# The last feed-forward network's output: seven block products in place of eight

## The chip, the cores and the metric

One core of one Trainium2 chip runs the whole kernel in one launch. The metric is the device time of that launch in microseconds (us). The profile is one profiled execution; times inside it count from its first instruction.

## The reference

One transformer-like layer over 512 latent tokens and 256 context tokens, 1024 features wide:

```
x  = x + position embedding
x  = LN(a*x + 0.5*gate*swiglu(modulate(x)))      # network 1, context tokens too
x  = LN(a*x + gate*mixer(modulate(x), context))  # gated linear attention and HGRN2, both directions
x  = LN(a*x + 0.5*gate*swiglu(modulate(x)))      # network 2, latent tokens: the change is here
swiglu(h) = (silu(h @ Wg) * (h @ Wu)) @ Wout     # 1024 -> 2816 -> 1024
```

All in float32, with `a` = 2 ** 0.25; `gate` is one row of 1024 factors, applied to the output columns. So the last network computes hid (512 x 2816) times Wout (2816 x 1024).

## The kernel before

All of it is one list of weight jobs (`weight_jobs`, `JOBS`), which every engine walks in the same order: network 1 for latent tokens (`L1`), for context tokens (`C`), the mixer, then network 2 for latent tokens (`L2`). A matmul operand in float32 is split in a high part (float32r) and a low part, the rest; a product is three matmuls, low x high, high x low and high x high (`product`, L1962 to L1964).

A weight job goes through four engines. SP loads 1 MB (or 0.75) into one of two raw buffers (`load`; buffer i % 2, as soon as VectorE has made the low part of job i - 2). ScalarE copies the high part (`split_hi`, L839) into one of three slots, when TensorE is done with the job before in that slot. VectorE subtracts for the low part (`split_lo`, L1291). TensorE waits for the low part (`ready`).

Network 2 ran in two parts of 11 hidden tiles (`FFN_PARTS`). An inner job ("in") computes gate and up columns of one tile of 128 hidden features for 512 tokens: 48 matmuls of 512 columns into a pair of PSUM banks. ScalarE takes the silu (L899), VectorE multiplies (L1462), ScalarE copies the high part (L904) and VectorE the low part (L1468) of the hidden tile. Then the output jobs ("out") of that part: for each half of the 1024 output columns, three steps of 3, 4 and 4 k tiles, and in each step all four token tiles (`out_half`). VectorE multiplies a finished bank by the gate row (L1406) and adds it to `xl` (`add_output`, L1412, L1414). For the last half the gate was multiplied into the raw weights instead (`gate_weights`, L1301), and TensorE took the tiles in an order of their own (`LAST_ORDER`, `last_half`), so that each tile's statistics (L1343, L1346), centring (L1384), scaling (L1391) and store can follow while TensorE works on the next.

The order on each engine is written out by hand, and an engine waits in order: what stands behind a waiting instruction waits too. GpSimd's queue is idle in this stage. PSUM has eight banks of 512 floats; the inner jobs use 0 to 3 (and 4 for one early tile).

Of the kernel before, what the change touches and what calls it, by code (L numbers as in the profile page):

```python
# [38 lines left out]
FFN_PARTS = {"L1": (11, 11), "C": (22,), "L2": (11, 11)}  # L46
OUT_STEPS = {11: (3, 4, 4), 22: (4, 4, 4, 4, 3, 3)}
LAST_ORDER = [(0, 0), (0, 1), (0, 2), (0, 3), (1, 0), (1, 1), (2, 0), (2, 1), (1, 2), (2, 2), (1, 3), (2, 3)]
# [11 lines left out]
def weight_jobs():  # L60
# [3 lines left out]
    def ffn(tag):  # L64
        for part, tiles in enumerate(FFN_PARTS[tag]):
            jobs.extend((tag, "in", part, j) for j in range(tiles))
            jobs.extend((tag, "out", part, half, s) for half in range(2) for s in range(len(OUT_STEPS[tiles])))
# [33 lines left out]

USES = [sum(slot_of(j) == slot_of(i) for j in range(i)) for i in range(len(JOBS))]
# [11 lines left out]


def gated(i):

    return i < len(JOBS) and JOBS[i][:4] == ("L2", "out", 1, 1)
# [27 lines left out]
def out_keys(tag):  # L146

    tiles = TC if tag == "C" else TL
    return [(tag, part, half, i) for part in range(len(FFN_PARTS[tag])) for half in range(2) for i in range(tiles)]

# [41 lines left out]
def build(nc, t, out):  # L192

    with ExitStack() as ctx:
# [8 lines left out]
        h_hi = sb("h_hi", [P, KT, TOK], F32R)  # L203
        h_lo = sb("h_lo", [P, KT, TOK], F32R)
# [29 lines left out]
        with ExitStack() as s0:  # L234
# [7 lines left out]
            with ExitStack() as s3:  # L242
# [22 lines left out]
                with ExitStack() as s1:  # L265
                    hid_last = [sb(f"hid_{x}_last", [P, 11, W], F32R, s1) for x in ("hi", "lo")]
                    gate_last = sb("gate_last", [KT, P], F32, s1)
# [7 lines left out]
        for block in (xc, gain_bias_b):  # L275
            ada_slots.append(block[:, :, :].rearrange("p a (b c) -> p (a b) c", c=256))
        sums = small[:, 0:3 * (TL + TC)].rearrange("p (a b) -> p a b", b=3)
# [33 lines left out]

        gate_dram = nc.dram_tensor("gate_rows", (4, KT, P), F32, kind="Internal").ap()
# [60 lines left out]
        def hidden_of(tag):  # L373

            return {"L1": hid_lat, "C": hid_ctx, "L2": hid_last}[tag]
# [60 lines left out]

        def weight_size(i):

            key = JOBS[i]
            if key[1:2] == ("out",):  # L440
                return out_k(key[0], key[2], key[4])[1] * W
            return {"LR": KT * 32, "mix": SLOT // 2, "early": SLOT // 2}.get(key[0], SLOT)

        def weights(i):
# [3 lines left out]
            if JOBS[i] == ("LR",):  # L448
                return (raw[i % 2][:, 0:KT * 32],) + tuple(x[s][:, 0:KT * 96] for x in (hi, lo))
            return tuple(x[:, 0:weight_size(i)] for x in (raw[i % 2], hi[s], lo[s]))  # L450
# [19 lines left out]
        s_smask = sem("scan_mask_loaded")  # L470
# [4 lines left out]
        s_ones = sem("ones_loaded")  # L475
# [22 lines left out]
        s_sum = sem("centred_squares_summed")  # L498
# [19 lines left out]
        s_fmod = sem("first_h_tile_modulated")  # L518
# [18 lines left out]
        s_a2hi = sem("a2_hi_ready")  # L537
# [11 lines left out]
        s_ez = sem("gla_exp_ready")  # L549
# [3 lines left out]
        s_le = sem("forget_log_ready")  # L553
# [7 lines left out]
        s_eq = sem("exp_q_ready")  # L561
        s_ei = sem("exp_k_ready")
        s_ex = sem("exp_tail_ready")
        s_fac = sem("chunk_factors_ready")
# [20 lines left out]
        s_gated = sem("last_half_weights_gated")  # L585
        s_se = sem("silu_exp_ready")
        s_sc = sem("silu_exp_plus_one_ready")
        s_sl = sem("silu_log_ready")
# [9 lines left out]
        w2o = t["ffn2_w_out"].rearrange("(k p) n -> p k n", p=P)  # L598
        wmi = t["w_mix_in"].rearrange("(k p) n -> p k n", p=P)
# [19 lines left out]

        block = ctx.enter_context(nc.Block())  # L620
# [3 lines left out]
        def _(sp):  # L624
            def load(i, pieces=2):
                key, s = JOBS[i], i % 2
                raw = weights(i)[0]
                if i >= 2:
                    sp.wait_ge(s_lo[slot_of(i - 2)], USES[i - 2] + 1)
                if key[0] == "V" and key[1] == 0:  # L630
                    pass
                if key[1:2] == ("in",):
# [6 lines left out]
                    return  # L639
                if key[1:2] == ("out",):  # L640
# [3 lines left out]
                    src, c0, width = (w2o if tag == "L2" else w1o), half * W, W  # L644
# [42 lines left out]
            sp.dma_start(smask[:, :], t["k_smask"][:, 0:SEQ]).then_inc(s_smask, 16)  # L687
# [15 lines left out]
            for i in range(4, len(JOBS)):  # L703
# [6 lines left out]
                if key == ("mo", 0, 1):  # L710

                    sp.wait_ge(s_ex, n2(len(GROUPS) - 1, 1))
# [18 lines left out]
        def _(pool):  # L731
# [25 lines left out]
            pool.wait_ge(s_smask, 16)  # L757
# [28 lines left out]
            def state_queries(g, d):  # L786

                pool.wait_ge(s_qdec, n2(g, d))
                pool.wait_ge(s_fac, n2(g, d))
# [27 lines left out]

        @block.scalar
        def _(act):
            def wait_done(i):  # L820
                act.wait_ge(s_done[slot_of(i)], USES[i] + 1)

            def split_hi(i):
# [10 lines left out]
                if gated(i):  # L834
                    act.wait_ge(s_gated, JOBS[i][4] + 1)
# [12 lines left out]
            def centred_std(what, stream, s, i):  # L848
# [3 lines left out]
                nc.scalar.activation(between_sq[:, :], x_of(stream, i), ACT.Square, bias=mv[:, c, 0:1], scale=-1.0,  # L852
                                     accum_out=mv[:, c, 1:2]).then_inc(s_sum, 1)
                act.wait_ge(s_sum, n - STAT["post", "ctx", 0, 0] + 1)
# [33 lines left out]
            def ffn(tag):  # L888
# [3 lines left out]
                for part, tiles in enumerate(FFN_PARTS[tag]):  # L892
                    for j in range(tiles):
                        i, idx = JOB[tag, "in", part, j], HID[tag, part, j]
                        if i not in (0, L2_FIRST):
# [11 lines left out]
                    for half in range(2):  # L907
                        for s in range(len(OUT_STEPS[tiles])):
                            split_hi(JOB[tag, "out", part, half, s] + 2)
                            between(tag, b)  # L910
                            b += 1

# [79 lines left out]
            for pair in range(4):  # L992
# [4 lines left out]
                for k in (2 * pair, 2 * pair + 1):  # L997
                    if k >= 2:
                        act.wait_ge(s_hk, k - 1)
                    nc.scalar.activation(mod_k[:, k % 2, :], xnT[:, k, :], ACT.Identity, bias=mods[:, KT + k, 0:1],  # L1000
                                         scale=scale1[:, k, 0:1]).then_inc(s_fmod, 1)
                    act.wait_ge(s_fmod, k + 1)
# [55 lines left out]
            def forget_sigmoid(g, d):  # L1058
                act.wait_ge(s_e1, FG[g, d] + 1)
                nc.scalar.activation(X0, X0, ACT.Ln).then_inc(s_le, 1)  # L1060
                act.wait_ge(s_le, FG[g, d] + 1)
# [14 lines left out]
            def gla_log(g, d):  # L1076
                act.wait_ge(s_abs, Z[g, d] + 1)
                nc.scalar.activation(X0, X0, ACT.Exp, scale=-1.0).then_inc(s_ez, 1)
                act.wait_ge(s_ez, Z[g, d] + 1)
# [1534 lines left out]
```

## Time and profile before

| | us |
|---|---|
| runs, median of 3 (lowest, highest) | 1347.28 (1345.25, 1348.06) |
| span of the profiled execution | 1344.9 |
| TensorE busy (share of the span) | 1323.4 (98%) |
| VectorE busy | 801.2 (60%) |
| ScalarE busy | 517.5 (38%) |
| GpSimd busy | 74.2 (6%) |

TensorE is PE in the views, its weight loads PEld, VectorE is DVE, ScalarE is ACT, GpSimd is POOL, SyncE is SP; an engine's name with a q is its queue issuing DMAs. Matmuls overlap, so their starts tell the pace better than their durations.

### The profile page before, as it was taken

What the parts mean: (1) busy time and instruction counts of PE and PEld (TensorE: products, weight loads), DVE (VectorE), ACT (ScalarE), POOL (GpSimd) and SP (SyncE); (2) the same over time, 40 slices, a digit from 0 to 9 for tenths busy, and PEclk for the clock granted to TensorE, in tenths of its full rate; (3) what the DMA queues carried; (4) which work ended last, traced back from release to release, by engine and by line L of the source; (5) the groups of instructions that cost most, each with busy time, mean ns of one, the idle gap of its engine ahead of it and who ended that gap; (6) DMA issues with size and microseconds to landing.
All of it is one profiled execution on the core that took longest, in us unless ns stands there. A gap on an engine that the chain in (4) does not pass through costs nothing.

```text
span 1344.9 us, 17714 instructions
## 1 busy us (share of the span) xinstructions
PE 1323.4 (98%) x7200; PEld 1116.1 (83%) x7200; DVE 801.2 (60%) x1146; ACT 517.5 (38%) x718; POOL 74.2 (6%) x83
## 2 busy tenths in 40 slices
PE   8999999999999999999999999999999999999997
PEld 5778888888889999888888788887898888888886
DVE  5546588666777776565136878777863333433356
ACT  5535211222213544566235655556652231222211
POOL 1000000000000000000001111110000000000000
PEclk8999999999999999999999999999999999999999
DMA  9965545665455676552022112123335333333211
GB/s 319 285 177 175 195 151 157 190 186 180 151 178 147 190 188 189 173 172 94 23 79 64 48 48 63 48 64 114 107 85 159 94 103 97 96 101 105 86 63 63
DMA packets 206400, 175.00 MB, mean 130 GB/s; under 512 B 6906, under 2 KB 175464, under 8 KB 206320
## 3 DMA queue, kind: packets, MB, share of 16 engines
q1 hardware_dynamic: 197816, 142.74, 36.6%
q0 software_dynamic: 7808, 29.46, 6.6%
q10 hardware_dynamic: 696, 1.68, 0.4%
q8 instruction: 57, 0.93, 0.3%
q14 instruction: 23, 0.19, 0.0%
HBM read 171.74 MB, written 2.11 MB: 129 GB/s over the span
## 4 chain that ended last, share of the span: by engine, by line
PE 89%; DVE 5%; ACT 3%; issue 2%; DMA 1%; ACTq 0%; DVEq 0%; SPq 0%
PE ps L1962 28%; PE ps L1964 27%; PE ps L1963 27%; PE ps L2001 1%; DVE w_lo L1291 1%; PE ps L2413 1%; PE ps L2398 1%; DMA w_raw<-ffn_w_in 1%; PE ps L2161 0%; PE ps L2014 0%; PE ps L2432 0%; PE ps L2184 0%; DVE xl L1384 0%; DVE xl L1433 0%; PE ps L2205 0%
## 5 line engine op out<-in xcount | busy, mean ns | idle before, releaser
L1962 PE MATMUL ps<-h_hi,w_lo 128*128 128x512 f32 (+1 forms) x1120 | 391.4, 349 | 2.1 <-DVE h_lo L1584 1.0
L1964 PE MATMUL ps<-h_hi,w_hi 128*128 128x512 f32 (+1 forms) x1120 | 387.8, 346 | 0.0
L1963 PE MATMUL ps<-h_lo,w_hi 128*128 128x512 f32 (+1 forms) x1120 | 387.6, 346 | 0.0
L1291 DVE TENSOR_TENSOR w_lo<-w_raw,w_hi 128x2048 fp32r<-128x2048 f32 (+1 forms) x107 | 237.1, 2218 | 169.8 <-ACT w_hi L839 169.7
L839 ACT ACTIVATE w_hi<-w_raw 128x2048 fp32r<-128x2048 f32 (+1 forms) x107 | 198.3, 1854 | 344.9 <-PE ps L1964 315.4
L1962 PEld LDWEIGHTS ps<-h_hi,w_lo 128*128 128x128 f32 x1120 | 211.7, 189 | 32.5 <-issue 5.3
L1964 PEld LDWEIGHTS ps<-h_hi,w_hi 128*128 128x128 f32 x1120 | 211.7, 189 | 26.9
L1963 PEld LDWEIGHTS ps<-h_lo,w_hi 128*128 128x128 f32 x1120 | 211.8, 189 | 25.5
L1313 DVE SCALAR_TENSOR_TENSOR ada_row<-ada_block,c_cols,ada_row 128x256 f32<-128x256 f32 x224 | 108.6, 485 | 8.0
L1462 DVE TENSOR_TENSOR glu<-ps,glu 128x512 f32<-128x512 f32 (+1 forms) x66 | 39.4, 598 | 123.0 <-ACT glu L899 123.0
L1962 PE MATMUL ps<-h_hi,half_lo 128*128 128x512 f32 (+1 forms) x272 | 102.0, 375 | 0.7 <-ACT beside_lo L1123 0.4
L1964 PE MATMUL ps<-h_hi,half_hi 128*128 128x512 f32 (+1 forms) x272 | 97.6, 359 | 0.0
L1963 PE MATMUL ps<-h_lo,half_hi 128*128 128x512 f32 (+1 forms) x272 | 97.4, 358 | 0.0
L899 ACT ACTIVATE glu<-ps 128x512 f32<-128x512 f32 (+1 forms) x66 | 33.9, 514 | 146.8 <-PE ps L1964 146.8
L1962 PE MATMUL ps<-w_hi,hid_lo_lat 128*128 128x512 f32 x176 | 69.6, 396 | 0.0
L1964 PE MATMUL ps<-w_hi,hid_hi_lat 128*128 128x512 f32 x176 | 68.6, 390 | 0.0
L1963 PE MATMUL ps<-w_lo,hid_hi_lat 128*128 128x512 f32 x176 | 68.5, 389 | 0.0
L1962 PE MATMUL ps<-w_hi,hid_lo_last 128*128 128x512 f32 x176 | 68.5, 389 | 0.0
L1963 PE MATMUL ps<-w_lo,hid_hi_last 128*128 128x512 f32 x176 | 68.5, 389 | 0.0
L1964 PE MATMUL ps<-w_hi,hid_hi_last 128*128 128x512 f32 x176 | 68.5, 389 | 0.0
L1962 PEld LDWEIGHTS ps<-h_hi,half_lo 128*128 128x128 f32 x272 | 51.3, 189 | 10.4 <-issue 2.8
L1962 PE MATMUL ps<-w_hi,h_lo 128*128 128x512 f32 x144 | 57.0, 396 | 1.4 <-DVE w_lo L1291 1.4
(273 smaller groups left out, 1770.9 us busy)
## 6 DMA issues: line engine op xcount, KB each, us to landing
w_raw<-ffn_w_in SPq DMA_DIRECT2D x124, 512.0 KB, 5.3
w_raw<-ffn_w_out SPq DMA_DIRECT2D x60, 512.0 KB, 4.2
ada_block<-w_ada POOLq DMA_DIRECT2D x28, 1024.0 KB, 5.8
half_raw<-w_mix_in SPq DMA_DIRECT2D x48, 256.0 KB, 3.3
ada_block<-w_ada SPq DMA_DIRECT2D x6, 1024.0 KB, 9.5
w_raw<-ffn_w_in SPq DMA_DIRECT2D x32, 128.0 KB, 6.1
w_raw<-w_mix_in SPq DMA_DIRECT2D x8, 512.0 KB, 4.2
w_raw<-ffn_w_out SPq DMA_DIRECT2D x12, 256.0 KB, 4.1
```

Source lines behind the costliest of these rows:

```text
L839: nc.scalar.activation(hi, raw, ACT.Copy).then_inc(s_hi[s], 1)
L899: nc.scalar.activation(glu[:, j % 2, 0:n], ps[:, hidden_bank(tag, part, j), 0:n], ACT.Silu).then_inc(s_silu, 1)
L1291: nc.vector.tensor_tensor(lo, raw, hi.bitcast(F32), ALU.subtract).then_inc(s_lo[s], 1)
L1313: ins = nc.vector.scalar_tensor_tensor(out=row, in0=ada_block[:, k, :], scalar=c_cols[:, k, v:v + 1], in1=row, op0=ALU.mult, op1=ALU.add)
L1462: nc.vector.tensor_tensor(hf, ps[:, hidden_bank(tag, part, j) + 1, 0:n], hf, ALU.mult).then_inc(s_hf, 1)
L1962: nc.tensor.matmul(dst, s_low, m_high, start=start, stop=False)
L1963: nc.tensor.matmul(dst, s_high, m_low, start=False, stop=False)
L1964: return nc.tensor.matmul(dst, s_high, m_high, start=False, stop=stop)
L2001: ins = nc.tensor.matmul(ada_sums_ps[:, j, v, :], ada_row[:, v, c], ones[:, 0:2], start=True, stop=True)
L2398: ins = nc.tensor.matmul(ps[p0:p0 + pn, 5, slot * P:(slot + 1) * P], ktok[:, j, p0:p0 + pn], vtok[:, tile, v], start=j != 1, stop=j != 0, ...
L2413: ins = nc.tensor.matmul(ps[:, o_bank(g, hd), c], St[p0:p0 + pn, order(d).index(tile), :], QST[d][p0:p0 + pn, c], start=d == 0 and tile == ...
```

## The change

The output product of network 2 is cut in 2 x 2 x 2 blocks: two token halves, two halves of the 2816 hidden features, two halves of the 1024 columns. In place of the eight block products (A11 B11 + A12 B21 and so on) it computes seven, by the scheme of Strassen and Winograd, from sums of blocks:

- All 22 inner jobs run first; `hid_last` keeps the hidden tiles as plain float32, without the split in two.
- Activation sums are made by VectorE in place: one subtraction of 256 columns with each inner job from the twelfth on, and nine subtractions of up to 1024 elements (`left_n2`, `left_s4`, `left_s3`) during the first products.
- Weight sums (`WEIGHT_SUMS`, four of them, 1408 x 512 floats each) are made in device memory: GpSimd issues four plain copies and four accumulating DMAs from the third inner job on, each waiting for those it needs. SP waits for a sum's semaphore before it loads its first piece.
- Each product has three steps of 4, 4 and 3 k tiles and two token tiles: 21 jobs. For each job ScalarE and VectorE split both the left block (`left_high`, `left_low`) and the weights.
- P1 with P6, P7 and P4 accumulate one after another in one pair of banks (4, 5), P5 with P3 in another (6, 7), P2 in a third (0, 1). Between them ScalarE copies P1, P5 and P3's banks out (`keep`), and VectorE adds or subtracts what a pair of banks holds to these copies (`join`, `add_joined`). TensorE waits for a copy or a join before it adds to the bank (`seven_free`).
- The gate multiply is back on the output for all tiles; `gate_weights` goes.
- Statistics of a row tile need both of its column halves: tiles 0 and 1 are complete after P2, tiles 2 and 3 after P4. Centring of tiles 0 and 1 is placed in step 16, scaling in step 18.
- In the diff below, the pieces stand in this order: constants, SP, GpSimd, ScalarE, VectorE, TensorE (`seven_free`).
- Outside this stage several semaphores are merged (the exponentials of the mixer count in one, ScalarE gets a chain semaphore like VectorE's, `ones` and the scan mask share one), with the same order of work.

```diff
-FFN_PARTS = {"L1": (11, 11), "C": (22,), "L2": (11, 11)}
+FFN_PARTS = {"L1": (11, 11), "C": (22,), "L2": (22,)}
+SEVEN = ("P1", "P5", "P3", "P6", "P2", "P7", "P4")
+SEVEN_STEPS = (4, 4, 3)
+SEVEN_BANKS = {"X": (4, 5), "Y": (6, 7), "Z": (0, 1)}
+SEVEN_SUM = {"P1": "X", "P6": "X", "P7": "X", "P4": "X", "P5": "Y", "P3": "Y", "P2": "Z"}
+LAST_ORDER = [(0, 0), (0, 1), (1, 0), (2, 0), (1, 1), (2, 1)]
...
+                    if key[2] in WEIGHT_SUMS:
+                        sp.wait_ge(s_wsum, 16 * WEIGHT_SUMS.index(key[2]) + 16)
+                        src = w_sums[WEIGHT_SUMS.index(key[2])]
...
+                    for a, b in ((0, 2), (2, kk)):
+                        sp.dma_start(raw[:, a:b, :], src[:, k0 + a:k0 + b, :]).then_inc(s_loaded[s], 16)
...
+            pool.wait_ge(s_hf, HID["L2", 0, 2] + 1)
+            copy_weights("P5", corner(0, 0))
+            copy_weights("P7", corner(0, 1))
+            pool.wait_ge(s_wcopy, 32)
+            add_weights("P5", corner(0, 1))
+            copy_weights("P6", corner(1, 1))
+            pool.wait_ge(s_wsum, 16)
+            add_weights("P7", corner(1, 1))
+            copy_weights("P4", corner(1, 0))
+            pool.wait_ge(s_wsum, 32)
+            pool.wait_ge(s_wcopy, 64)
+            add_weights("P6", sum_dram[WEIGHT_SUMS.index("P5")])
+            pool.wait_ge(s_wsum, 48)
+            add_weights("P4", sum_dram[WEIGHT_SUMS.index("P6")])
...
+                for n in range(3 * len(SEVEN)):
+                    p, s = JOBS[SEVEN_FIRST + n][2:]
+                    if n in (3, 6, 9):
+                        keep(SEVEN[n // 3 - 1], 1)
+                    split_both_hi(n + 2)
+                    if n in (2, 5, 8):
+                        keep(p, 0)
...
+                for n in range(3 * len(SEVEN)):
+                    p, s = JOBS[SEVEN_FIRST + n][2:]
+                    before = SEVEN[n // 3 - 1]
+                    if s == 0 and before in ("P6", "P2", "P7") and n:
+                        join(before, 1)
+                        add_joined(before, 1)
+                    split_both_lo(n + 2)
+                    if n in (1, 2, 3):
+                        left_n2(n - 1)
+                        left_s4(n - 1)
+                    if n in (7, 8, 9):
+                        left_s3(n - 7)
+                    if s == 2 and p in ("P6", "P2", "P7"):
+                        join(p, 0)
+                        add_joined(p, 0)
+                    if n == 16:
+                        for i in range(2):
+                            post_center("lat", 2, i)
+                    if n == 18:
+                        for i in range(2):
+                            post_scale("lat", 2, i)
+                for tile in range(2):
+                    add_joined("P4", tile)
+                    post_center("lat", 2, 2 + tile)
+                    post_scale("lat", 2, 2 + tile)
...
+                if p in ("P6", "P3"):
+                    pe.wait_ge(s_kept, (2 if p == "P3" else 0) + tile + 1)
+                if p in ("P7", "P4"):
+                    pe.wait_ge(s_joined, (4 if p == "P4" else 0) + tile + 1)
```

## Rows read from the trace of the kernel before

**Rows 1.** The page: busy time of each engine; its chain of work that ended last.

```profile
PE 1323.4 (98%) x7200; PEld 1116.1 (83%) x7200; DVE 801.2 (60%) x1146; ACT 517.5 (38%) x718; POOL 74.2 (6%) x83
...
PE 89%; DVE 5%; ACT 3%; issue 2%; DMA 1%; ACTq 0%; DVEq 0%; SPq 0%
```

**Rows 2.** Stretches: length, engines' busy us, granted clock, DMA share, GB/s.

```profile
1217.00:1277.00 60.00, 60.00 (x266) 49.70 (x265) 19.20 (x16) 14.75 (x15) 0.00 (x0) 1.00 0.32 97
...
1277.00:1337.30 60.30, 60.24 (x266) 49.57 (x264) 37.29 (x39) 10.53 (x10) 0.00 (x0) 1.00 0.15 53
```

**Rows 3.** Timeline, TensorE, last output half: start us, duration us, instruction.

```profile
1330.28 0.39 PE L1962 MATMUL ps<-w_hi,hid_lo_last 128*128 128x512 f32 x1
...
1336.85 0.39 PE L1964 MATMUL ps<-w_hi,hid_hi_last 128*128 128x512 f32 x1
```

**Rows 4.** Timeline, ScalarE then VectorE, last two inner jobs.

```profile
1266.56 0.60 ACT L899 ACTIVATE glu<-ps 128x512 f32<-128x512 f32 x1 [7.44 <-PE ps L1964]
...
1268.52 1.90 ACT L839 ACTIVATE w_hi<-w_raw 128x2048 fp32r<-128x2048 f32 x1
1277.44 0.60 ACT L899 ACTIVATE glu<-ps 128x512 f32<-128x512 f32 x1 [7.02 <-PE ps L1964]
...
1270.46 2.29 DVE L1291 TENSOR_TENSOR w_lo<-w_raw,w_hi 128x2048 fp32r<-128x2048 f32 x1 [1.11 <-ACT w_hi L839]
```

**Rows 5.** Timeline, VectorE, last token tile after TensorE's end.

```profile
1337.34 0.69 DVE L1414 TENSOR_TENSOR xl<-xl,ps 128x512 f32<-128x512 f32 x1
1338.06 0.69 DVE L1343 BATCH_NORM_STATS2 last_stats<-xl 128x6 f32<-128x512 f32 x1
1338.79 0.21 DVE L1346 BATCH_NORM_AGGREGATE mv<-last_stats 128x2 f32<-128x12 f32 x1
1339.03 1.28 DVE L1384 SCALAR_TENSOR_TENSOR xl<-xl,mv,gain_bias_b 128x1024 f32<-128x1024 f32 x1
1340.35 0.17 DVE L1352 RECIPROCAL rstd<-std 128x1 f32<-128x1 f32 x1
1340.55 1.28 DVE L1391 SCALAR_TENSOR_TENSOR xl<-xl,rstd,gain_bias_b 128x1024 f32<-128x1024 f32 x1
```

**Rows 6.** Timeline, ScalarE and VectorE: one instruction of each size priced.

```profile
989.43 1.06 ACT L876 ACTIVATE h_hi<-h_full 128x1024 fp32r<-128x1024 f32 x1
...
988.05 1.22 DVE L1377 TENSOR_TENSOR h_lo<-h_full,h_hi 128x1024 fp32r<-128x1024 f32 x1
...
1285.65 1.49 ACT L839 ACTIVATE w_hi<-w_raw 128x1536 fp32r<-128x1536 f32 x1 [4.34 <-PE ps L1964]
...
1287.17 1.76 DVE L1291 TENSOR_TENSOR w_lo<-w_raw,w_hi 128x1536 fp32r<-128x1536 f32 x1 [1.88 <-ACT w_hi L839]
```

**Rows 7.** DMA issues (KB each, median us to landing), one issue pair, landing of weights.

```profile
w_raw<-ffn_w_in SPq DMA_DIRECT2D x124, 512.0 KB, 5.3
w_raw<-ffn_w_out SPq DMA_DIRECT2D x60, 512.0 KB, 4.2
...
gain_bias_b<-ln_bias SPq DMA_DIRECT2D x3, 512.0 KB, 7.6
...
1288.96 0.88 SPq L658 DMA_DIRECT2D w_raw<-ffn_w_out  x2
...
DMA to landing us min/median/max: 3.3/4.2/7.7
```

**Rows 8.** DMA queues in one us: GpSimd's at 213:214, SP's at 1013:1014 (packets, MB).

```profile
q0 software_dynamic: 96, 0.39, 107.7%
...
q1 hardware_dynamic: 662, 0.33, 111.7%
```

**Rows 9.** DMA queues in 102.70:103.40, both with work: packets, MB, share.

```profile
q0 software_dynamic: 28, 0.11, 63.6%
q1 hardware_dynamic: 115, 0.05, 32.7%
```

More of the change, by code:

```diff
@@ L8 @@
+import itertools
 from contextlib import ExitStack
@@ L66, in ffn @@
             jobs.extend((tag, "in", part, j) for j in range(tiles))
+            if tag == "L2":
+                jobs.extend((tag, "seven", p, s) for p in SEVEN for s in range(len(SEVEN_STEPS)))
+                continue
             jobs.extend((tag, "out", part, half, s) for half in range(2) for s in range(len(OUT_STEPS[tiles])))
@@ L146, in out_keys @@
 def out_keys(tag):
+    if tag == "L2":
+        return [(tag, 0, half, i) for half, tiles in ((1, (0, 1)), (0, (0, 1)), (1, (2, 3)), (0, (2, 3))) for i in tiles]
     tiles = TC if tag == "C" else TL
@@ L449, in weights @@
                 return (raw[i % 2][:, 0:KT * 32],) + tuple(x[s][:, 0:KT * 96] for x in (hi, lo))
+            if JOBS[i][1:2] == ("seven",):
+                p, step = JOBS[i][2:]
+                hi, lo = (x[s][:, 0:weight_size(i)].rearrange("p (k c) -> p k c", c=W) for x in (hi, lo))
+                return raw[i % 2][:, 0:weight_size(i)].rearrange("p (k c) -> p k c", c=W), hi, lo
             return tuple(x[:, 0:weight_size(i)] for x in (raw[i % 2], hi[s], lo[s]))
@@ new lines, in left_s3, with product_done, join @@
+            def left_s3(s):
+                dve.wait_ge(s_leftlo, seven_number("P3", s) + 1)
+                left_sum("P7", s, "P6", "P4")
+            def product_done(p, tile):
+                if tile:
+                    wait_done(JOB["L2", "seven", p, 2])
+                else:
+                    dve.wait_ge(s_seven, SEVEN.index(p) + 1)
+            def join(p, tile):
+                early = {"P6": "P3", "P2": "P1", "P7": "P5"}[p]
+                product_done(p, tile)
+                dve.wait_ge(s_kept, 2 * ("P1", "P5", "P3").index(early) + tile + 1)
+                y = early_sum[early, tile]
+                nc.vector.tensor_tensor(y, y, seven_bank(p, tile), ALU.add if p == "P2" else ALU.subtract
+                                        ).then_inc(s_joined, 1)
@@ new lines, in add_joined @@
+            def add_joined(p, tile):
+                rows, half = output_of(p)
+                i, c = 2 * rows + tile, slice(half * W, (half + 1) * W)
+                if p == "P4":
+                    product_done(p, tile)
+                    y = seven_bank(p, tile)
+                else:
+                    dve.wait_ge(s_joined, 2 * ("P6", "P2", "P7").index(p) + tile + 1)
+                    y = early_sum[{"P6": "P3", "P2": "P1", "P7": "P5"}[p], tile]
+                dve.wait_ge(s_gate, 16 * GATE["lat", 2] + 16)
+                x = halves(xl[:, i, c])
+                link(nc.vector.tensor_tensor(y, y, halves(gate_b[:, c]), ALU.mult))
+                nc.vector.scalar_tensor_tensor(out=x, in0=x, scalar=ALPHA, in1=y, op0=ALU.mult, op1=ALU.add).then_inc(s_yev, 1)
+                half_statistics(i, half)
@@ L2122, in ffn, with last_ffn @@
+            def last_ffn():
+                for j in range(3, 22):
+                    hidden("L2", 0, j, 0, SEQ)
+                    between("L2", j)
+                for p in SEVEN:
+                    for s, tile in LAST_ORDER if p == SEVEN[-1] else itertools.product(range(3), range(2)):
+                        seven_products(p, s, tile)
             def ffn(tag):
```

318 lines of the change are left out of this document (206 added, 112 removed).

## The prediction, made before the changed kernel was run

> **What bounds the kernel now.** I read the page's busy shares and its chain first: TensorE is busy 98% and holds 89% of the chain [rows 1]. Then the table by stretches, for the inner and the output jobs of the last network: TensorE busy 60.00 of 60.00 us and 60.24 of 60.30 us, granted clock 1.00 (its 2.4 GHz level), while VectorE is busy 19.20 and 37.29 us [rows 2]. So the stage that the change touches has no gap on TensorE, and its time is the number of matmuls times their pitch. The timeline gives the pitch: 29 matmuls of 512 columns start between 1330.28 and 1336.85 us, 0.2266 us each, though one lasts 0.39 us [rows 3]; they overlap, so the pitch is the price, not the duration. An inner job is 48 of them, 10.88 us, as two silus in turn show [rows 4].
>
> **What the products save.** Before: 22 k tiles x 4 token tiles x 2 halves = 176 products of three matmuls = 528. After: 7 x 11 x 2 = 154 products = 462. 66 fewer x 0.2266 = 14.96 us less. The inner jobs are the same 22, only without the output jobs between them. The last output half starts at 1337.08 - 59.8 = 1277.2 us now (1337.08: last start plus a pitch [rows 3]); with the 59.8 us of the first part's output jobs gone from between the inner jobs, the seven products start at about T = 1277.2 - 59.8 = 1217.4 us. I give times of the new stage from T. Unstalled it ends at T + 104.7; now VectorE ends at 1340.55 + 1.28 = 1341.83 = T + 124.4 [rows 5].
>
> **What has to keep up.** An old output step of four k tiles fed four token tiles (10.88 us); a new one feeds two: 5.44 us (4.08 us for three k tiles). Per step ScalarE makes the left high part (1024 elements, 1.06 us) and the weights' high part (1.90, or 1.49 for 1536); VectorE the left low part (1.28, as the 1024-element scalar_tensor_tensor; the plain subtraction took 1.22) and the weights' low part (2.29 or 1.76) [rows 4 to 6]. A raw buffer's cycle: two DMAs issued over 0.88 us, the second landing about 0.44 + 4.2 after the low part that freed it, then 1.90 and 2.29: 8.9 us, for two steps that last 9.5 to 10.9 [rows 4, 6, 7]. That holds by 1 us. ScalarE needs at most 3.0 of 5.44 us and has only six bank copies (about 0.6 each, as a silu of 512) more. VectorE: low parts 68; nine left sums, 10; six joins at 0.69 and their gate, add and statistics (0.73 + 0.72 + 0.73, starts in rows 5), 17; the early centring and scaling of two tiles, 5.6. That is 101 us, less 7 done before T, on 104.7: nearly full, and not even. For a product with joins it is 9.8 + 2 x 2.9 = 15.6 us against 14.96.
>
> **Where that stalls TensorE.** I laid the four instruction lists out in order, each instruction at the later of its engine being free and its waits. Through P6 nothing stalls: TensorE ends it at T + 59.9. VectorE finishes the low parts of step 13 (steps counted from 0) at 61.2, joins both tiles of P6 (66.8), splits step 14 (69.4) and 15 (72.8). Buffer 16 was asked for at 69.5, lands 74.1, high part 76.0, low part 78.4. Then P2's two joins, with statistics (84.7), and step 17's parts: 87.3. TensorE wanted step 17 at 85.7: stall 1.7. Next is the clearest place: in the loop body, step 19 is split and two tiles are centred before P7's first tile is joined, and P4 accumulates in the bank that this join reads. Step 18's low part ends 90.7, the centrings 93.3; buffer 19 was freed at 87.3, landed 92.0, high part 93.9, low part 96.7; join 97.3; P4 starts 97.4, where P7 ended 91.4: stall 6.0. The wait is queued behind a split that itself waits for a DMA. P4 then runs 14.96 us, to 112.5. VectorE, still with step 20 and two scalings, reaches P4's first tile at 108.0 and ends the second at 118.3, 5.8 us behind TensorE instead of 4.7, since the gate multiply is back (0.73) and it comes late.
>
> Sum: -14.96 + 1.7 + 6.0 + 1.1 = -6.1 us. The profiled execution's span of 1344.9 becomes about 1338.8; the median of the runs, 1347.28, lies 2.4 above the span, and I keep that distance: **1341.1 us**. A landing of 3.3 us makes the gain 7.0, one of 5.3 makes it 4.4. Were my VectorE queue too pessimistic, the gain goes to 14.96 - 0.5 for the gate multiply.
>
> **What the trace doesn't show: sums in device memory.** Four copies and four accumulating transfers of 1408 x 512 floats, 2.88 MB each, from GpSimd's queue, started after the third inner job, near 1012 us; ordered by waits, copies partly beside adds. No accumulating DMA is in the trace. Fast end: GpSimd's queue moved 0.39 MB in 1 us [rows 8], 7.4 us for one plus about 2: 75 us in all. Slow end: the slowest 512 KB transfer, 7.6 us, 69 GB/s [rows 7]: 42 us each, 334 in all. P5's sum (three transfers) is asked for near T - 5, 200 us after the start; P6's (seven) at T + 31, 237 us after. The point is 85 GB/s. I take near the fast end for copies, since the queue and size are those of the row, and twice that for adds, which read two operands: 120 us, over before T. Then its cost on the path is zero.
>
> It also shares the 16 DMA engines with the inner loads. Their cover: low part ends 1272.75, the same buffer's next high part starts at 1268.52 + 21.76: 17.5 us, of which 0.4 + 5.3 are used [rows 4, 7]. So a load may take three times as long for nothing. The trace has only tails of overlap: in 0.70 us both queues moved 28 packets of 4 KB and 115 of 0.5 KB [rows 9], about four small for each large one. Loads would halve their speed, not more.
>
> The Trainium skill ("DMA: Bandwidth & Descriptors", Queues, rings and completion order) says each engine alternates between queue rows packet by packet; the row above doesn't look like one for one, but its overlap is short. The same notes ("Collectives: The Full Stack") call a reduce step two reads and one write. By the first, loads would starve; that is rival 3.
>
> Edits at nothing: merged semaphores (the same order of increments; VectorE's wait for the mask is on data that landed long before), the linked copies (0.1 us).
>
> **Rivals.** (1) VectorE isn't late: the whole saving but the gate multiply, 1347.3 - 14.5 = 1332.8. For it: both 60-us stretches show VectorE under 63% busy. Against it: the layout above. Chance 0.17. (2) Loads of the new stage land slower at double the pace: at 6.2 us six waits appear and the gain is 0.2 (1347.5); at 7.7, the slowest shown, 10.7 lost (1358). Chance 0.10. (3) The slower side, first: packet-for-packet alternation. A load is 128 packets per engine; an engine passes 6 large packets of 4 KB per us (0.083 us for 2 KB) and 41 small (0.024) [rows 8]. Beside copies a load takes 128 x 0.107 = 13.7 us, beside adds at three times the work 35, both against 10.88 wanted. Over the 134 us of sums 5.5 of 12.3 loads arrive, 74 us short; cover absorbs 11.7 and two jobs' lead some 15: about 47 late, 1388. It decides once a load takes over 17.5 us. Chance 0.12. (4) Sums under 85 GB/s: P6's first load holds SP, and all loads behind it; at the slow end P6's sum is 56 us late, 1397. Chance 0.08. (5) That P4 or P7 isn't shorter in matmuls is excluded by the loop counts.
>
> **How the numbers follow.** Forecast 0.53, 1341.1, its own range 1337 to 1345. Range: 1332 (rival 1) to 1362, which takes in rival 2 and half of 3 and 4, leaving out some 0.1 above. A run of this kernel can tell 0.2%, 2.7 us. Faster: 0.17 + 0.50 less a little for forecasts near 1345 = 0.66; same 0.09; slower 0.25.
>
> **What would show it.** Right: TensorE matmuls down by 66 and no idle until P7; an idle of about 6 us before P4 that a VectorE join ends, and a shorter one before P7's last step; the last VectorE chain about 5.8 us behind TensorE; POOL's transfers landed before T. Wrong: idle on TensorE between 1012 us and T, released by low parts that wait for DMA (rival 3); a long SP wait on the sums (4); idle before P3 or P2 (2); TensorE full to the end (1).

## The result, and the profile after

| | us |
|---|---|
| before, median of 4 runs (lowest, highest) | 1347.24 (1345.25, 1348.06) |
| after, median of 4 runs | 1368.09 (1367.43, 1372.18) |
| ratio after / before, 95% interval | 1.0164 (1.015, 1.0179) |
| span of the profiled execution, before, after | 1344.9, 1366.4 |

The kernel became 1.6% slower. 1341.1 us was forecast, with a range of 1332 to 1362: the sign was wrong and the time lies outside the range. The page of after: busy time, chain, DMA issues (KB each, median us from issue to landing).

```profile
PE 1316.4 (96%) x7134; PEld 1109.1 (81%) x7134; DVE 830.7 (61%) x1165; ACT 541.6 (40%) x732; POOL 82.8 (6%) x91
...
PE 72%; DMA 9%; DVE 8%; SPq 4%; ACT 4%; issue 3%; DVEq 0%; ACTq 0%
...
weight_sums<-ffn_w_out POOLq DMA_DIRECT2D x6, 2816.0 KB, 27.4
...
weight_sums<-weight_sums POOLq DMA_DIRECT2D x2, 2816.0 KB, 19.3
```

TensorE has its 66 matmuls less (7200 in [rows 1]), but its share of the chain fell from 89% to 72%, and DMA holds 9% where it held 1%. The table by stretches, in the columns of [rows 2], says where:

```profile
1012.00:1040.00 28.00, 28.00 (x126) 23.17 (x125) 5.97 (x4) 3.17 (x4) 2.11 (x3) 1.00 1.01 326
...
1060.00:1080.00 20.00, 15.35 (x69) 12.21 (x67) 0.68 (x1) 2.40 (x2) 2.36 (x2) 0.95 1.07 258
1080.00:1100.00 20.00, 13.93 (x48) 11.02 (x48) 2.21 (x2) 1.16 (x1) 0.94 (x1) 0.76 1.03 285
...
1140.00:1160.00 20.00, 16.86 (x68) 13.83 (x69) 11.79 (x10) 7.28 (x7) 0.00 (x0) 0.91 0.60 160
1160.00:1240.00 80.00, 80.00 (x355) 66.24 (x354) 26.69 (x24) 18.71 (x16) 0.00 (x0) 1.00 0.32 94
1240.00:1320.00 80.00, 80.00 (x355) 66.24 (x354) 62.36 (x49) 45.95 (x40) 0.00 (x0) 1.00 0.52 176
```

TensorE has gaps from 1060 to 1160 us and none from 1160 to 1320. In the gaps its granted clock fell as well, to 0.76: between 1060 and 1160 us TensorE idles 18.6 us, and the slower matmuls make the rest of the delay. The DMA engines are busy all the time (1.01 to 1.07) from 1012 us on, where GpSimd's sums start, until they end near 1137. ScalarE's timeline names what was waited for, the inner loads (idle before, releaser in brackets):

```profile
1077.38 1.91 ACT L939 ACTIVATE w_hi<-w_raw 128x2048 fp32r<-128x2048 f32 x1 [23.46 <-DMA w_raw<-ffn_w_in]
1098.84 1.91 ACT L939 ACTIVATE w_hi<-w_raw 128x2048 fp32r<-128x2048 f32 x1 [19.07 <-DMA w_raw<-ffn_w_in]
...
1120.55 1.92 ACT L939 ACTIVATE w_hi<-w_raw 128x2048 fp32r<-128x2048 f32 x1 [15.91 <-DMA w_raw<-ffn_w_in]
```

From issue to landing each half of an inner load took 12.7 us at least, 17.1 at the median and 42.0 at most between 1012 and 1140 us, against 3.6 to 5.6 behind it. The last silu of the inner jobs starts at 1242.87 us, 25.3 later than the forecast's T of 1217.4 plus the 0.2 us that it follows TensorE.

The new stage then went nearly as it was laid out. Its two stalls, on TensorE and then on VectorE's queue:

```profile
1330.27 0.50 PE L2184 MATMUL ps<-w_hi,h_lo 128*128 128x512 f32 x1 [1.76 <-DVE w_lo L1433]
1340.52 0.76 PE L2184 MATMUL ps<-w_hi,h_lo 128*128 128x512 f32 x1 [5.87 <-DVE kept_sums L1669]
1341.08 0.63 PE L2185 MATMUL ps<-w_lo,h_hi 128*128 128x512 f32 x1
1341.50 0.63 PE L2186 MATMUL ps<-w_hi,h_hi 128*128 128x512 f32 x1
```

```profile
1333.46 2.60 DVE L1516 SCALAR_TENSOR_TENSOR xl<-xl,mv,gain_bias_b 128x1024 f32<-128x1024 f32 x2
...
1337.48 2.29 DVE L1433 TENSOR_TENSOR w_lo<-w_raw,w_hi 128x2048 fp32r<-128x2048 f32 x1 [0.16 <-ACT w_hi L939]
1339.69 0.68 DVE L1669 TENSOR_TENSOR kept_sums<-kept_sums,ps 128x512 f32<-128x512 f32 x1
...
1362.06 1.28 DVE L1523 SCALAR_TENSOR_TENSOR xl<-xl,rstd,gain_bias_b 128x1024 f32<-128x1024 f32 x1
```

The join (L1669) that P4 waits for stands behind the two centrings and the split of step 19, as forecast: 5.87 us, where 6.0 was said. What the layout did not have is the pace behind the stall: the matmuls start 0.43 us apart, not 0.2266; between 1340.5 and 1345.0 us the granted clock was 0.58, near the 1.2 GHz level. P4's 66 matmuls took 16.8 us instead of 14.96.

So after against before, in spans: 25.3 (inner stage late) - 6.1 (the new stage as forecast) + 2.3 (1.9 of it the slow clock behind the stall) = +21.5 = 1366.4 - 1344.9. What remained to be shown: that the sums' transfers make the inner stage late, by which mechanism, and whether the new stage is worth its 6 us.

### The profile page after: what moved, and what is told of

Same layout as the page of the kernel before. It is cut to its first block, busy times and chain, and to the rows that moved or that the text cites. A ratio compares the mean times of both kernels' runs of the same rounds, so it can differ in the third digit from the quotient of the medians.

```text
span 1366.4 us, 17701 instructions
## 1 busy us (share of the span) xinstructions
PE 1316.4 (96%) x7134; PEld 1109.1 (81%) x7134; DVE 830.7 (61%) x1165; ACT 541.6 (40%) x732; POOL 82.8 (6%) x91
## 4 chain that ended last, share of the span: by engine, by line
PE 72%; DMA 9%; DVE 8%; SPq 4%; ACT 4%; issue 3%; DVEq 0%; ACTq 0%
PE ps L2184 23%; PE ps L2186 22%; PE ps L2185 22%; DMA w_raw<-ffn_w_in 8%; DVE w_lo L1433 2%; ACT w_hi L939 2%; SPq L753 1%; SPq L696 1%; SPq L749 1%; PE ps L2223 1%; DMA w_raw<-weight_sums 1%; PE ps L2647 1%; SPq L765 1%; PE ps L2632 1%; DVE xl L1516 0%
## 5 line engine op out<-in xcount | busy, mean ns | idle before, releaser
L2184 PE MATMUL ps<-h_hi,w_lo 128*128 128x512 f32 (+1 forms) x1120 | 394.6, 352 | 20.0 <-DVE hid_last L1697 18.6
L1433 DVE TENSOR_TENSOR w_lo<-w_raw,w_hi 128x2048 fp32r<-128x2048 f32 (+1 forms) x116 | 256.3, 2210 | 235.9 <-ACT w_hi L939 235.6
L939 ACT ACTIVATE w_hi<-w_raw 128x2048 fp32r<-128x2048 f32 (+1 forms) x116 | 214.4, 1849 | 371.0 <-PE ps L2186 262.0
L2186 PEld LDWEIGHTS ps<-h_hi,w_hi 128*128 128x128 f32 x1120 | 213.3, 190 | 27.6
L2184 PE MATMUL ps<-w_hi,h_lo 128*128 128x512 f32 x298 | 117.9, 396 | 9.0 <-DVE kept_sums L1669 5.9
L2185 PE MATMUL ps<-w_lo,h_hi 128*128 128x512 f32 x256 | 100.4, 392 | 0.0
L2186 PE MATMUL ps<-w_hi,h_hi 128*128 128x512 f32 x256 | 100.3, 392 | 0.0
L2184 PEld LDWEIGHTS ps<-w_hi,h_lo 128*128 128x128 f32 x298 | 56.4, 189 | 22.2 <-issue 6.5
L1697 DVE TENSOR_TENSOR hid_last<-ps,glu 128x512 f32<-128x512 f32 x22 | 15.2, 689 | 88.2 <-ACT glu L1048 88.2
L2186 PEld LDWEIGHTS ps<-h_hi,half_hi 128*128 128x128 f32 x272 | 51.3, 189 | 7.9
```

The source lines that it names most:

```text
L939: nc.scalar.activation(hi, raw, ACT.Copy).then_inc(s_hi[s], 1)
L1433: nc.vector.tensor_tensor(lo, raw, hi.bitcast(F32), ALU.subtract).then_inc(s_lo[s], 1)
L1697: nc.vector.tensor_tensor(hid_last[:, j, :], ps[:, hidden_bank("L2", 0, j) + 1, :], glu[:, j % 2, :], ALU.mult).then_inc(s_hf, 1)
L2184: nc.tensor.matmul(dst, s_low, m_high, start=start, stop=False, skip_group_check=shared)
L2185: nc.tensor.matmul(dst, s_high, m_low, start=False, stop=False, skip_group_check=shared)
L2186: return nc.tensor.matmul(dst, s_high, m_high, start=False, stop=stop, skip_group_check=shared)
```

## The experiments

Ratios are to the kernel before on the same chip, with 95% intervals. Theory A is rival 3's mechanism, packets in turn; B is the new order of the inner stage itself; C is a shared rate of bytes.

**no_sums.** The sums are not formed, and SP loads a plain corner of the weights in place of each; everything else stays, so the time is meant and not the output.

```diff
-                        sp.wait_ge(s_wsum, 16 * WEIGHT_SUMS.index(key[2]) + 16)
-                        src = w_sums[WEIGHT_SUMS.index(key[2])]
+                        row, half = ((0, 0), (0, 1), (1, 1), (1, 0))[WEIGHT_SUMS.index(key[2])]
+                        src = w2o[:, 11 * row:11 * row + 11, half * W:(half + 1) * W]
...
-            copy_weights("P5", corner(0, 0))
-            copy_weights("P7", corner(0, 1))
...
```

> The changed kernel without any transfer from GpSimd's queue: the four weight sums are not formed, and SP loads a plain corner of the weights in place of each (so the output is not the reference's); all other instructions stay. Theory A (GpSimd's packets alternate with SP's 0.5 KB packets and starve the inner loads, 25.3 us, and the clock fell in the gaps that this made): no wait for loads between 1012 us and T, loads land in 5 us, T at 1217 to 1218, the new stage as laid out, 1340 to 1344 us. Theory B (the new inner stage itself is late, since 22 inner jobs now stand in a row without output jobs between them, so that both raw buffers turn at the full pace): the gaps stay, 1362 to 1369 us.

Measured: 1342.55 us, 0.9974 (0.9963 to 0.9984). TensorE is busy 20.00 of every 20 us from 1040 to 1160, and P4 starts 24.9 us earlier than in after, behind the same stalls:

```profile
1305.60 0.50 PE L2159 MATMUL ps<-w_hi,h_lo 128*128 128x512 f32 x1 [1.80 <-DVE w_lo L1408]
1315.60 0.76 PE L2159 MATMUL ps<-w_hi,h_lo 128*128 128x512 f32 x1 [5.63 <-DVE kept_sums L1644]
```

B is out: the transfers make the whole delay. The new stage is worth 3.5 us (2.2 to 5.0), not 6.1: P4's 66 matmuls took 17.7 us in this trace, 2.8 more than at full clock, and 6.1 - 2.8 = 3.3. That trace is of the slowest of the eight runs (1344.58 us). Behind the same stall P4 took 1.9 us more in after, 2.9 in sums_small_packets and 1.5 in sums_paced, so the clock takes 1.5 to 2.9 us off the 6.1, and 3.2 to 4.6 remain.

**sums_in_before.** The same eight transfers in the kernel before, for nobody's use.

```diff
+            pool.wait_ge(s_hf, HID["L2", 0, 2] + 1)
+            copy_weights("P5", corner(0, 0))
+            copy_weights("P7", corner(0, 1))
...
```

> The kernel before, with the same four copies and four accumulating transfers of 2.88 MB added from GpSimd's queue at the same point, for nobody's use. Theory A: the inner jobs of the first part (until about 1098 us) lose 11 to 20 us, as the changed kernel had lost some 11 of TensorE's time by 1100 us and more with the clock; the output jobs behind them load in 2 KB rows, 32 packets per engine in place of 128, so they keep up beside the same traffic with landings of 7 to 9 us: 1358 to 1368 us. Theory B: 1347 us. Theory C (the transfers share bytes of device memory, not packets): inner and output loads are slowed alike, by 1 MB each at the same rate, and the loss goes on through the output jobs until 1137 us.

Measured: 1373.63 us, 1.0206 (1.0192 to 1.0219), 27.6 us lost, above the 1358 to 1368 us of A. The inner jobs lost their share (one wait of ScalarE for a load is 24.06 us), but the output jobs behind them, which I expected to keep up with their 2 KB rows, waited too, 10.33 and 11.85 us. Queues in 1114:1118 us, where the sums were in an adding transfer from one sum to the next (packets, MB, share of 16 engines):

```profile
q0 software_dynamic: 82, 0.67, 80.5%
q1 hardware_dynamic: 82, 0.17, 12.6%
q10 hardware_dynamic: 36, 0.15, 8.9%
```

That transfer's packets are 8.2 KB (0.67 MB / 82), larger than any that A's sum had used, and a 2 KB row of an output load waits for one of them just as a 0.5 KB row does: 20 rows per us, so 512 of them take 25 us. C had foreseen a loss in both stages, A's arithmetic had not; the next view decides between them.

**The packets, counted in slices of 4 us in after.** First copies (1020:1024), then adds from the weights (1052:1056), adds from sum to sum with a third queue at work (1112:1116), the same alone with SP (1124:1128), and the end of the last transfer (1136:1140):

```profile
q0 software_dynamic: 317, 1.30, 88.8%
q1 hardware_dynamic: 319, 0.16, 14.9%
...
q0 software_dynamic: 321, 0.66, 89.2%
q1 hardware_dynamic: 322, 0.16, 20.9%
...
q0 software_dynamic: 80, 0.66, 79.5%
q10 hardware_dynamic: 80, 0.33, 20.3%
q1 hardware_dynamic: 80, 0.04, 5.1%
...
q0 software_dynamic: 98, 0.80, 96.2%
q1 hardware_dynamic: 98, 0.05, 6.3%
...
q1 hardware_dynamic: 2296, 1.15, 109.0%
q0 software_dynamic: 15, 0.02, 3.1%
```

While both queues have work, they send equally many packets, whatever the sizes: 317 and 319 at 4.1 and 0.5 KB, 321 and 322 at 2.1 KB, 98 and 98 at 8.2 KB; with a third queue 80, 80 and 80. The bytes stand as 8 to 1, 4 to 1 and 16 to 1, so they are not what is shared. SP's pace is then set by the other's packet: about 80 per us beside copies and adds from the weights (an inner load of 2048 packets: 25.6 us; slices beside copies range from 63 to 88), 24 per us beside the 8 KB adds (84 us). Between two transfers SP is alone and catches up at 574 per us. Without other traffic the stage takes 189 per us (4160 packets in 22 us, 1170 to 1192).

The Trainium skill ("DMA: Bandwidth & Descriptors", Queues, rings and completion order) says that each DMA engine takes the queue rows in turn, a whole packet of each. By that rule the counts are equal, and they are. How many of the profile's packets make one turn, the counts don't show.

**sums_small_packets.** Each transfer issued as four of 1408 x 128 floats; the adds lose their argument `max_dma_last_dim=8192` with it.

```diff
-                pool.dma_start(sum_dram[WEIGHT_SUMS.index(p)], source, accum_op=ALU.add, max_dma_last_dim=8192).then_inc(s_wsum, 16)
+                for c in range(0, W, P):
+                    pool.dma_start(sum_dram[WEIGHT_SUMS.index(p)][:, c:c + P], source[:, c:c + P], accum_op=ALU.add).then_inc(s_wsum, 16)
```

> The changed kernel, the same sums at the same place, but each transfer issued as four of 1408 x 128 floats, so that the pieces are 0.5 KB in place of some 4 KB. Theory A (one packet for one packet): an inner load of 128 packets per engine waits for 128 small ones, 128 x 2 x 0.024 = 6 us and at most 10 with reads and writes of the adds, under the cover of 17.5: the inner stage is on time or nearly, sums take longer (17 us each for copies, up to 35 for adds, 140 to 210 in all, near the point where P5 or P6 would wait): 1340 to 1352 us. Theory C (bytes of device memory are shared): as many bytes, so the same 25 us late: 1362 to 1369 us.

Measured: 1343.2 us, 0.998 (0.9971 to 0.9989), as good as without any sums, with as many bytes (23.07 MB) moved between 1012 and 1180 us. Queues in 1075:1095:

```profile
q0 software_dynamic: 3527, 1.99, 73.3%
q1 hardware_dynamic: 3526, 1.78, 44.7%
```

Again one for one, but GpSimd's packets are now 0.56 KB on average, and SP gets 176 per us: a load in 11.6 us, against 10.88 wanted, a shortage that the cover takes. TensorE has no gap until 1304 us. Only the adds became small; the copies still moved in packets of about 4 KB (0.68 MB in 180 packets in 1020:1022). C, which had this run at 1362 to 1369, is out.

**sums_paced.** The large transfers of the change, unchanged in size, one at a time, each behind the next second inner job; their order changes too, each add comes right behind its own copy.

```diff
-            pool.wait_ge(s_hf, HID["L2", 0, 2] + 1)
+            def after_tile(j):
+                pool.wait_ge(s_hf, HID["L2", 0, j] + 1)
+
+            after_tile(2)
             copy_weights("P5", corner(0, 0))
+            after_tile(4)
+            pool.wait_ge(s_wcopy, 16)
+            add_weights("P5", corner(0, 1))
+            after_tile(6)
             copy_weights("P7", corner(0, 1))
...
```

> The changed kernel with its own eight large transfers (pieces of 2 to 8 KB, as in the change), but one at a time: each waits for the next second inner job, every 21.8 us from the third job on, so that each burst of 14 to 19 us is followed by some undisturbed microseconds. Same bytes, same packets, same starving within a burst. Theory A with the cover of the inner loads: in a burst SP gets 78 to 82 packets per us where 188 are wanted, so 15 us leave 1600 packets, 0.8 load or 8.7 us, short; the cover of 11.7 us takes that, and the gap lets it recover. No wait on TensorE in the inner stage, or at most 3 us: 1342 to 1347. Rival (what counts is the sum of overlapped time, 125 us of it, however it is cut): 25 us late as before, 1362 to 1369.

Measured: 1342.87 us, 0.9974 (0.9963 to 0.9984). TensorE's table:

```profile
1080.00:1100.00 20.00, 20.00 (x90) 16.57 (x89) 3.68 (x3) 3.03 (x3) 0.88 (x1) 1.00 1.11 236
...
1120.00:1140.00 20.00, 20.00 (x90) 16.56 (x89) 5.95 (x5) 3.20 (x3) 0.94 (x1) 1.00 0.96 204
```

The same bytes in the same packets (23.07 MB in 6464 in both runs), in flight for 14 to 22 us each, and nothing is lost. ScalarE waited for a load twice, 3.01 and 2.94 us, within the cover. SP had so far caught up between the bursts that part of each found it with little to send (25 packets in 1078:1084 us). So a burst costs nothing as long as the loads it holds back fit in the cover and the next one leaves room to catch up. In after the transfers follow each other at once, 125 us long; in them SP sent 16028 packets where 189 per us ask for 23,600: 3.7 loads or 40 us short, of which 25 us reached TensorE.

**sums_in_mixer, mixer_small_packets.** The eight transfers moved into the mixer (copies after 640 us, adds from 664 us on), large and in small pieces.

```diff
+            pool.wait_ge(s_wcopy, 32)
+            add_weights("P5", corner(0, 1))
+            copy_weights("P6", corner(1, 1))
             plus_one(0, "gate0")
             plus_one(0, "gate1")
             state_queries(0, 0)
+            pool.wait_ge(s_wsum, 16)
+            add_weights("P7", corner(1, 1))
+            copy_weights("P4", corner(1, 0))
```

> The changed kernel with the same eight transfers moved forward into the mixer stage (copies from 640 us, adds from 700 us on), where SP loads 0.5 MB for each 11 us. Theory A: a load of half the size, at the landing of 17 us for 1 MB that was seen, takes 8.5 us and stays under 11; the network's inner loads run alone again: 1340 to 1346 us, faster than before by 0.1 to 0.5%. Rival: the mixer's many small steps are tied to small transfers and to loads of its own, and the delay only moves: 1350 to 1368 us.

> sums_in_mixer with the transfers in the small pieces of sums_small_packets. Theory A (what cost 12 us in the mixer was the same starving of SP's 0.5 KB rows, by the adds' 2 and 8 KB packets): the loss falls to less than 4 us, 1342 to 1347. Rival (in the mixer it is something else, such as small transfers that sit behind the sums' bytes): 1352 to 1357 us as before.

Measured: 1354.89 us, 1.0063 (1.005 to 1.0075), and 1354.92, 1.0069 (1.0055 to 1.0083). Both rivals won. The waits of the two between 660 and 880 us (us in total, times, longest), the first line from the large pieces, the others from the small:

```profile
ACT half_hi L938 <- DMA half_raw<-w_mix_in: 11.3, 4, 5.8
```

```profile
POOL weight_sums L847 <- issue: 29.3, 2, 14.7
ACT gate L1293 <- POOL gate L866: 23.9, 6, 17.1
...
ACT half_hi L940 <- DMA half_raw<-w_mix_in: 3.8, 1, 3.8
```

The loads' share did fall with the packets, from 11.3 to 3.8 us. But the mixer has GpSimd compute, and its instructions stand behind the transfers that it issues. With four pieces for each, GpSimd sat 14.6 us ahead of the fourth of a group (725.7 to 740.3) while earlier ones were still under way, and ScalarE's gate, which waits for GpSimd, sat 17.1. In the inner jobs the same pauses (19.9 us ahead of 1068.37) hold up nobody. The chain of mixer_small_packets runs through that pause. That the queue was full is argued, the trace names no releaser; how the 12 us of the large pieces divide is open.

**join_first.** On top of sums_small_packets, both joins of P7 ahead of the split of step 19, the centrings behind the split of step 20.

```diff
+                    if n == 17:
+                        join("P7", 0)
+                        join("P7", 1)
                     split_both_lo(n + 2)
...
-                    if n == 16:
+                    if n == 18:
                         for i in range(2):
                             post_center("lat", 2, i)
```

> On top of sums_small_packets one edit on VectorE: both joins of P7 stand before the split of step 19, and the centring of tiles 0 and 1 moves behind the split of step 20. Tells whether the stall before P4 is what costs the time, or VectorE's total. Theory A (the wait order made the stall): no stall of 5.9 us before P4's first matmul. By the same layout as in the prediction TensorE would end 2.7 us earlier (T + 109.8), with a stall of 3.4 us inside P4 for the low part of step 20, and VectorE, which is full from T + 61 on, would end at T + 118.6 where the layout without the edit gives 118.3: no time won by that, and only the clock that fell behind the long stall comes back, 2 to 3 us: 1340 to 1343 us. Rival (the stall alone is the cost): 1334 to 1337 us.

Measured: 1342.07 us, 0.997 (0.9959 to 0.9982). The stall before P4 is gone, one of 3.41 us for the low part of step 20 stands inside P4 (3.4 in the layout), and the end hardly moved. The clock that should have come back did so in small part only: behind this stall too the matmuls start 0.43 us apart, and P4 took 2.0 us more than at full clock. So the stall before P4 was a mark of VectorE's load, not a cost of its own.

**vector_order.** VectorE's order from P6 on laid out anew, nothing added or removed.

```diff
+                    if n in (12, 17):
+                        if n == 17:
+                            join("P7", 0)
+                        join(("P6", "P7")[n == 17], 1)
                     split_both_lo(n + 2)
+                    if n == 12:
+                        add_joined("P6", 1)
+                    if n == 15:
+                        join("P2", 1)
+                        add_joined("P2", 1)
...
+                    if n == 16:
+                        post_center("lat", 2, 0)
+                    if n == 17:
+                        post_center("lat", 2, 1)
+                        post_scale("lat", 2, 0)
+                        add_joined("P7", 0)
+                    if n == 18:
+                        add_joined("P7", 1)
+                        post_scale("lat", 2, 1)
```

> On top of sums_small_packets VectorE's order is laid out anew from P6 on: P6's second join before the split of step 14 and its addition behind it, the split of step 17 before P2's second join, both joins of P7 before the split of step 19, and the centring, scaling and additions spread into the waits behind steps 16 to 20. No instruction added or removed. By the layout: no stall before P7's last step, 0.8 us before P4, 3.2 before its second step, TensorE ends at T + 108.7, VectorE at T + 115.6, 2.7 us sooner than the layout gives for the order as it is, and some 3 us of clock back: 1336 to 1340 us. Rival (VectorE is not what ends the chain, and the order does not matter): as sums_small_packets, 1343.

Measured: 1338.5 us, 0.9945 (0.9932 to 0.9959), 4.7 us under sums_small_packets: 2.7 in the layout, and the clock, which cost 0.4 us here and 2.9 there. The two stalls left are nearly those of the layout (0.8 and 3.2):

```profile
1307.56 0.47 PE L2195 MATMUL ps<-w_hi,h_lo 128*128 128x512 f32 x1 [0.80 <-DVE kept_sums L1671]
1318.83 0.50 PE L2195 MATMUL ps<-w_hi,h_lo 128*128 128x512 f32 x1 [2.85 <-DVE w_lo L1435]
```

**vector_relieved, vector_relieved2.** As vector_order, and GpSimd normalises row tiles 0 and 1; in the second, VectorE doesn't wait for it and it starts earlier.

```diff
+                        nc.gpsimd.tensor_scalar(x, x, mv[:, c, 0:1], rstd[:, c:c + 1], ALU.subtract, ALU.mult)
+                        nc.gpsimd.tensor_tensor(x, x, gain_b[:, :], ALU.mult)
+                        nc.gpsimd.tensor_tensor(x, x, bias_b[:, :], ALU.add)
```

> As vector_order, and the normalising of row tiles 0 and 1 (four instructions of 1.28 us on VectorE) is done by GpSimd instead, as six instructions of 1024 elements during P4. By the layout TensorE has no stall left and ends at T + 104.7, VectorE at T + 111.1: 1328 to 1332 us, 1.1 to 1.4% faster than the kernel before. Rival: GpSimd is slower than 2 us for one of the six, or slows VectorE beside it, and tiles 0 and 1 come last: 1336 us or more.

> vector_relieved with what the trace of that run showed mended: VectorE no longer waits for GpSimd's tiles before its own last two (it sat idle for 10.1 us), and ScalarE's roots and the reciprocals for tiles 0 and 1 stand one step earlier, so that GpSimd starts its 19.5 us at T + 89 in place of T + 95. By those durations GpSimd ends at T + 109, VectorE, with P4's first tile from T + 101 or 102 on and 10.5 us for two tiles, at T + 112: 1333 to 1336 us, 2 to 5 us under vector_order. Rival: GpSimd beside VectorE slows it or its tiles come last: 1338 or more.

Measured: 1343.58 us, 0.9984 (0.9975 to 0.9993), and 1338.66, 0.9949 (0.9935 to 0.9962). TensorE did as laid out: no stall, and its last matmul starts at 1322.78 and 1320.88 us (1325.53 in vector_order). In the first, VectorE sat idle 10.07 us for GpSimd's tiles, by a wait that I had put there. In the second it had no wait, and yet ended 12.2 us behind TensorE. VectorE and GpSimd side by side in vector_relieved2:

```profile
1308.09 2.28 DVE L1452 TENSOR_TENSOR w_lo<-w_raw,w_hi 128x2048 fp32r<-128x2048 f32 x1
...
1316.44 2.88 DVE L1704 SCALAR_TENSOR_TENSOR xl<-xl,kept_sums 128x512 f32<-128x512 f32 x1
...
1320.68 0.69 DVE L1704 SCALAR_TENSOR_TENSOR xl<-xl,ps 128x512 f32<-128x512 f32 x1
...
1325.18 3.04 DVE L1542 SCALAR_TENSOR_TENSOR xl<-xl,rstd,gain_bias_b 128x1024 f32<-128x1024 f32 x1
```

```profile
1305.41 11.01 POOL L924 TENSOR_SCALAR xl<-xl,mv,rstd 128x1024 f32<-128x1024 f32 x2 [144.42 <-DVE rstd L1729]
...
1316.38 5.19 POOL L926 TENSOR_TENSOR xl<-xl,gain_bias_b 128x1024 f32<-128x1024 f32 x2
```

Beside GpSimd's two-tensor instructions VectorE's additions of two SBUF tensors took 2.88 in place of 0.69 and 3.04 in place of 1.28 us; the one that reads PSUM kept its 0.69. The layout had priced each engine alone, and both runs missed what it gave (1328 to 1332 and 1333 to 1336 us).

**paced_and_order.** sums_paced with vector_order.

> Both mends together: the sums' large transfers one at a time as in sums_paced, and VectorE's order of vector_order. The two touch different stages, so their gains add: the inner stage on time (T at 1214 to 1218 us), no stall over 3 us in the new stage, 1336 to 1339 us, 0.5 to 0.7% faster than before. Rival (the two interact, as sums that end later than in the change meet the new stage's loads): 1341 or more.

Measured: 1338.62 us, 0.9943 (0.993 to 0.9957), the same as vector_order with small pieces. Both beat the kernel before by 0.6% and after by 2.2% (0.9943 / 1.0164).

## Why the prediction was wrong, step by step

**The saved products** (-14.96): right. 66 matmuls fewer, and no gap in the new stage until P7.

**VectorE's load and the stalls** (+1.7, +6.0, +1.1): right to 0.2 us each in after: 1.76, 5.87, and VectorE's end 5.8 us behind TensorE's. The reading was off in one point: the text called the stall before P4 "the clearest place", as though its order made the loss. join_first took it away and won little; vector_order spread the work and won 4.7 us over sums_small_packets.

**A term that was missing**: the clock. The sum priced every matmul behind a stall at 0.2266 us. P4's cost 1.9 us more in after, and 1.5 to 2.9 more in the four traces with this stall. With it the new stage is worth 3.2 to 4.6 us; no_sums measured 3.5.

**The sums' duration** (120 us, over before T): right, 125 us, from 1011.5 to 1137, but in part by luck. One at a time, in sums_paced, a copy took 14.4 to 16.6 us, not some 9, and an add 17.3 to 22.3, as estimated; 137 us in all, of which after saved some by running copies beside adds. Rival 4 is out, no load waited for a sum.

**The cover** of 17.5 us less what is used: right for a load held up now and then, sums_paced ran within it. "Three times as long for nothing" doesn't hold for a row of loads: one is wanted every 10.88 us, so each may take only twice its 5.7 us for long.

**Their weight on the inner loads**: this step failed. "Loads would halve their speed, not more" rested on 28 large and 115 small packets in 0.70 us, read as four small for one large. The same stretch in two parts, 102.70:103.00 and 103.00:103.40, in the kernel before:

```profile
q0 software_dynamic: 9, 0.04, 64.3%
q1 hardware_dynamic: 85, 0.04, 57.5%
...
q0 software_dynamic: 19, 0.08, 63.1%
q1 hardware_dynamic: 30, 0.01, 14.0%
```

The ratio runs from 9 to 1 down to 1.6 to 1 within it, and in its last 0.1 us SP sends one packet against six: the window held one queue's start and the other's end, and its mean said nothing of the rate once both were busy. That SP's surplus came over engines on which it was still alone is argued; no view splits a queue by engine. The rule of the Trainium skill ("DMA: Bandwidth & Descriptors", Queues, rings and completion order) stood in the prediction against this row; the slices of after shown above, in which both queues are busy, agree with it to 1%. The rule was right and the row was misread. So a load beside the sums took 25.6 us or more where the prediction had about twice its 5.3, and the cost put at zero was 25 us.

**Rival 3** had the mechanism, the place and the sign, at a chance of 0.12 and 1388 us. Its size was off both ways. Beside copies a load takes 25.6 us, not 13.7, since a packet of 4.1 KB takes 0.18 us of an engine (88.8% of 64 engine-us for 317), where 0.083 was used; beside adds of 2 KB packets 25, not 35; beside 8 KB packets 84, of which nothing was known. But the transfers have pauses between them, in which SP catches up at 574 packets per us. In all 3.7 loads were missing, not 6.8, and 25 us came through, not 47.

Rivals 1 and 2 are out: VectorE did stall TensorE, and the new stage's loads landed in 3.4 to 6.4 us, 3.9 at the median. The range ended at 1362 because rivals 3 and 4 were taken in by half; rival 3's own price was 1388.

## What to carry to other kernels

Before a large transfer is put beside a stream of loads, count packets, not bytes: the queues send equally many, so a load in 0.5 KB rows falls to the packet rate of the other queue, and the remedy is packets as small as the loads' own, or bursts that fit in the loads' cover. Read the rate of two queues from a stretch in which both are busy throughout. And where an engine is full, moving one wait shows another: lay out its whole queue, and add to each stall the slow clock behind it.

## What the runs showed of the hardware

- Two and three DMA queues with work send equally many packets, to within 1% in the slices shown, at 0.5 KB against 2.1, 4.1 and 8.2 KB. An add from one sum to the next inside device memory (with `max_dma_last_dim=8192`) moved in packets of 8.2 KB, an add from the weights with the same argument in 2.1 KB, plain copies in some 4 KB even when cut in columns of 512 bytes.
- SP's issuing is slowed beside such traffic as well: between 1012 and 1140 us one issue of a load took 4.2 us at the median and 14.9 at most in after, where two take 0.88 [rows 7].
- After a stall of 5.9 us TensorE started matmuls 0.43 us apart for 3.5 us (granted clock 0.58 over 4.5 us, near its 1.2 GHz level); after one of 3.4 us in join_first likewise (0.57 over 4 us), and P4 took 2.0 us more than at full clock. In vector_order, with stalls of 0.8 and 2.9 us, the clock stayed at 1.00, and P4 took 15.4 us without the stall, 0.4 more.
- The Trainium skill ("SBUF — State Buffer", SBUF: two separate sides) says that VectorE and GpSimd share a pair of ports, locked for a whole instruction, when VectorE reads two SBUF tensors beside a GpSimd instruction that reads SBUF. Beside GpSimd's two-tensor instructions that agrees, 2.88 against 0.69. Beside its tensor_scalar a product of 512 elements took 1.52 us in place of 0.69, but VectorE's subtractions of 2048 elements kept their time (2.28 us, as alone), which the rule alone doesn't explain; no run here tells why.
